# A twelve-layer token mixer in one launch: wide VectorE steps in the rwkv layers, key norms and key factors on ScalarE, and the closed block of the selective layer left out

## The chip, the cores and the metric

One core of a Trainium2 chip. The metric is the device time in microseconds of one execution of the whole program, median over the runs.

## The reference, cut to what matters

The input is 256 tokens of 1024 channels. Twelve sublayers follow one another, each adding its result to `x`: rwkv, ffn, stick-breaking attention, ffn, selective attention ("dsa"), ffn, rwkv, ffn, and then twice a mixed attention ("multi") and a gated ffn. Every sublayer begins with an RMS norm. All of it is float32.

```python
def rms_norm(x, g):
    y = xf * lax.rsqrt(jnp.mean(xf * xf, axis=-1, keepdims=True) + RMS_EPS)
    return (y * g).astype(x.dtype)

# rwkv, the parts that the change touches
shifted = jnp.pad(h, ((0, 0), (1, 0), (0, 0)))[:, :-1]
xm = h[:, :, None, :] + (shifted - h)[:, :, None, :] * mix        # six mixes
kk = heads(k * k_k)
kk = kk * lax.rsqrt(jnp.maximum(jnp.sum(kk * kk, axis=-1, keepdims=True), 1e-24))
k = k * (1.0 + (a - 1.0) * k_a)

# selective attention, 64 queries at a time
visible = kpos[None, :] < ((qpos // 64 + 1) * 64)[:, None]
score = sum over 8 index heads of wi * relu(qi . ki)              # where visible
top_val, top_idx = lax.top_k(score, 64)
p = softmax(q . k over the chosen keys);  o = p . v
```

The first 128 queries can see only the first 128 keys. So one block of 128 queries by 128 keys of every score matrix of the selective layer is closed.

## The kernel before, in words

Activations lie with channels on the 128 partitions, as eight tiles of 256 tokens. A "unit" is one weight block of 128x1024 that SyncE loads into a ring of four (`ring_a`). ScalarE writes its rounded high half (`hi`, L2026) and VectorE the remainder (`lo`, L2135) to `w_split`, and TensorE multiplies the unit in 24 matmuls: high by high, high by low, low by high, for eight tiles of channels (L1931 to L1933, in the rwkv layer's unit 0 L288 to L290, output units of attention L1353 to L1355). Each engine has its program written out in order; semaphores join them. The order by hand decides everything: an instruction waits until all those before it on its engine are through.

**Norm of an rwkv layer.** ScalarE squares the eight tiles of `x` (L2049), TensorE sums all eight with a matrix of ones (L1918), ScalarE takes ln and exp for the inverse root (L2034, L2036), VectorE multiplies `x` by gain and inverse root, tile by tile (L2148). GpSimd subtracts each token from its predecessor (L1142, L1143). VectorE forms the mixes in pairs of tiles (L868), ScalarE the high half of a pair (L639), VectorE the low half (L875). TensorE takes unit 0 pair by pair as they come. The waits for the large constant table stand behind this norm on TensorE, ScalarE and VectorE.

**Key norms.** While units 0 to 7 (the keys) run, ScalarE squares them. TensorE gathers sums by head (L297). ScalarE takes the square root (L657), with a table of its own, then the tanh of the decay ranks (L659), the high halves of mix pairs 2 and 3, and the ranks' high half (L665). VectorE clamps (L912) and inverts (L914); TensorE spreads the result back later. Unit 9 waits for the four pairs of group 3; the small matmuls of the decay (L319 to L321) wait for the ranks.

**Key factors.** After the gates, VectorE forms `1 + (a - 1) * k_a` and multiplies the keys, two instructions per tile of channels (L989, L992), with three unit splits between them.

**The selective layer.** 30 units are projected in "slots", then eight output units follow in slots 30 to 42. In slot n TensorE runs unit n and then what the pairs of heads need by then: norm and rope of queries and keys (L1271, L1273), turning values (L1280), scores (L1296), turning probabilities (L1309), the value product (L1320). In a slot VectorE does, in this order: index rope, normalise the first head of a pair, rope norms, shift and take maxima of a score pair (L1706, L1712), unit splits, normalise the second head (L1718, L1722), the low half of a pair's output (`out_low`, L1729), index sums, the top-eight steps, and last the evacuation of unit n (L1630). Eight steps, each two maxima of eight and two replacements (L1682, L1686), make the 64 chosen keys: one each in slots 9 to 14, with a second one in 10 and 13; the mask follows in slot 14. ScalarE squares a head pair (L1475, L1476) once its unit is evacuated. A later unit shares its PSUM bank with a value product, so it waits for `out_low` of that pair. Scores, probabilities and index scores are 512 columns: two blocks of 128 queries by 256 keys.

## Time and profile before

| | us |
|---|---|
| median of 3 runs | 2387.6 |
| lowest, highest | 2386.41, 2393.24 |
| the profiled execution | 2389.38 |
| its span, first to last instruction | 2387.6 |
| mean granted TensorE clock | 0.98 of full |

The profile is of one execution. PE is TensorE's matmuls, PEld its weight loads, DVE VectorE, ACT ScalarE, POOL GpSimd, SP SyncE. The profile names an instruction by engine and line, then the tile that it writes and those that it reads. In brackets stands how long the engine sat idle before it, and what released it.

### The profile page before, as it was taken

How to read it: one execution, taken by the hardware profiler on the slowest of the kernel's cores; microseconds unless marked ns; L12 is line 12 of the kernel's file. 1: busy time of each engine (PE TensorE's matmuls, PEld its weight loads, DVE VectorE, ACT ScalarE, POOL GpSimd, SP SyncE). 2: the span in 40 equal slices, each digit the busy share in tenths (PEclk: the TensorE clock that was granted, in tenths of full speed). 3: DMA queues.
4: the chain of work that ended last, by engine and by line, in shares of the span. 5: the costliest groups of instructions: out<-in, count | busy, mean ns of one | idle time of the engine just before them, and what ended most of it. 6: DMA issues, size and time to landing. Idle time of an engine off the chain costs nothing.

```text
span 2387.6 us, 55688 instructions
## 1 busy us (share of the span) xinstructions
PE 2251.9 (94%) x23028; PEld 2156.6 (90%) x23028; DVE 1568.9 (66%) x2402; ACT 1207.9 (51%) x2037; POOL 58.1 (2%) x83
## 2 busy tenths in 40 slices
PE   6899899999999989899988998999998999998998
PEld 5799799999999978799978998999897999887998
DVE  6854465566655688565588644655775777775776
ACT  5633454465544546454467334544675444675443
POOL 1000000000000010000010000000000000100000
PEclk8999999999999999999999999999999999998999
DMA  5310265533555433255523102555433554433653
GB/s 198 124 47 4 68 211 172 193 124 124 173 196 171 155 99 106 98 185 189 172 98 124 47 4 98 194 184 177 135 114 107 180 199 150 150 116 101 205 173 118
DMA packets 88437, 327.21 MB, mean 137 GB/s; under 512 B 9809, under 2 KB 9937, under 8 KB 87633
## 3 DMA queue, kind: packets, MB, share of 16 engines
q1 hardware_dynamic: 87984, 322.72, 40.2%
q8 instruction: 128, 2.10, 0.4%
q0 software_dynamic: 288, 2.10, 0.3%
q14 instruction: 37, 0.29, 0.0%
HBM read 323.73 MB, written 1.05 MB: 136 GB/s over the span
## 4 chain that ended last, share of the span: by engine, by line
PE 81%; DVE 10%; ACT 6%; issue 2%; ACTq 0%; DVEq 0%
PE bank L1931 15%; PE bank L1932 15%; PE bank L1933 15%; PE bank L1953 5%; PE bank L1954 5%; PE bank L1955 5%; DVE w_split L2135 2%; ACT w_split L2026 2%; PE bank L446 2%; PE bank L455 2%; PE bank L1353 1%; PE bank L1354 1%; PE bank L1355 1%; PE bank L469 1%; PE bank L1320 1%
## 5 line engine op out<-in xcount | busy, mean ns | idle before, releaser
L1931 PE MATMUL bank<-h_split,w_split 128*128 128x256 f32 x3176 | 912.2, 287 | 20.9 <-DVE h_split L2157 8.0
L1933 PE MATMUL bank<-h_split,w_split 128*128 128x256 f32 x3176 | 898.0, 283 | 0.0
L1932 PE MATMUL bank<-h_split,w_split 128*128 128x256 f32 x3176 | 897.9, 283 | 0.0
L2135 DVE TENSOR_TENSOR w_split<-ring_a,w_split 128x1024 fp32r<-128x1024 f32 x474 | 568.3, 1224 | 191.8 <-ACT w_split L2026 190.7
L1931 PEld LDWEIGHTS bank<-h_split,w_split 128*128 128x128 f32 x3176 | 602.4, 190 | 33.9 <-DVE h_split L2157 11.3
L1932 PEld LDWEIGHTS bank<-h_split,w_split 128*128 128x128 f32 x3176 | 598.3, 188 | 1.3
L1933 PEld LDWEIGHTS bank<-h_split,w_split 128*128 128x128 f32 x3176 | 597.0, 188 | 0.0
L2026 ACT ACTIVATE w_split<-ring_a 128x1024 fp32r<-128x1024 f32 x474 | 483.3, 1049 | 38.1 <-PE bank L1933 33.0
L1953 PE MATMUL bank<-act_split,d_split 128*128 128x256 f32 x1008 | 285.9, 284 | 3.8 <-DVE act_last L2218 2.4
L1954 PE MATMUL bank<-act_split,d_split 128*128 128x256 f32 x1008 | 285.5, 283 | 0.0
L1955 PE MATMUL bank<-act_split,d_split 128*128 128x256 f32 x1008 | 285.3, 283 | 0.0
L2097 ACT ACTIVATE work<-work 128x256 f32<-128x256 f32 x88 | 36.8, 419 | 347.8 <-DVE work L2196 347.8
L1953 PEld LDWEIGHTS bank<-act_split,d_split 128*128 128x128 f32 x1008 | 193.2, 192 | 5.0 <-DVE act_last L2218 2.8
L1955 PEld LDWEIGHTS bank<-act_split,d_split 128*128 128x128 f32 x1008 | 193.3, 192 | 0.0
L1954 PEld LDWEIGHTS bank<-act_split,d_split 128*128 128x128 f32 x1008 | 193.1, 192 | 0.0
L2196 DVE TENSOR_TENSOR work<-bank,work 128x512 f32<-128x512 f32 x132 | 91.0, 689 | 151.5 <-PE bank L1933 150.7
L2193 DVE TENSOR_TENSOR d_split<-ring_d,d_split 128x1024 fp32r<-128x1024 f32 x126 | 153.7, 1220 | 4.9 <-ACT d_split L2094 4.9
L2094 ACT ACTIVATE d_split<-ring_d 128x1024 fp32r<-128x1024 f32 x126 | 131.4, 1043 | 0.0
L2100 ACT ACTIVATE work<-work 128x256 f32<-128x256 f32 x44 | 18.4, 418 | 179.6 <-DVE work L2210 179.6
L1353 PE MATMUL bank<-o_split,w_split 128*128 128x256 f32 x256 | 80.7, 315 | 18.7 <-DVE o_split L1729 18.5
L2214 DVE TENSOR_TENSOR work<-work 128x256 f32<-128x256 f32 x132 | 56.2, 426 | 63.9 <-ACT work L2097 42.6
L2218 DVE TENSOR_TENSOR act_split<-work,act_split 128x256 fp32r<-128x256 f32 x126 | 53.6, 425 | 61.0 <-ACT act_split L2103 61.0
(273 smaller groups left out, 3263.9 us busy)
## 6 DMA issues: line engine op xcount, KB each, us to landing
ring_a<-wa SPq DMA_DIRECT2D x474, 512.0 KB, 3.9
ring_d<-wd SPq DMA_DIRECT2D x132, 512.0 KB, 4.4
tab_sb<-tab SPq DMA_DIRECT2D x1, 2448.0 KB, 13.4
hT<-na POOLq DMA_DIRECT2D x2, 1024.0 KB, 5.3
xT<-x SPq DMA_DIRECT2D x1, 1024.0 KB, 4.9
out<-xT SPq DMA_DIRECT2D x1, 1024.0 KB, 3.9
vec_sb<-vec SPq DMA_DIRECT2D x1, 288.0 KB, 4.9
tab_sb<-tab SPq DMA_DIRECT2D x1, 65.0 KB, 4.7
```

The source lines that it names most:

```text
L1353: mm(o, w[:, 0, ms], x[:, 0, k, :], start=(k == 0 and m % 2 == 0), stop=False, skip_group_check=True)
L1931: mm(dst, w[:, 0, ks], x[:, 0, k, :], start=(k == 0), stop=False)
L1932: mm(dst, w[:, 0, ks], x[:, 1, k, :], start=False, stop=False)
L1933: last = mm(dst, w[:, 1, ks], x[:, 0, k, :], start=False, stop=(k == KT - 1))
L1953: mm(o, w[:, 0, ms], x[:, 0, :], start=(first and m % 2 == 0), stop=False, skip_group_check=True)
L1954: mm(o, w[:, 0, ms], x[:, 1, :], start=False, stop=False, skip_group_check=True)
L1955: return mm(o, w[:, 1, ms], x[:, 0, :], start=False, stop=final, skip_group_check=True)
L2026: A(w_split[:, u % 4, 0, :], ring_a[:, u % 4, :], ACT.Copy).then_inc(s["w_hi"], 1)
L2094: A(d_split[:, q, 0, :], ring_d[:, q, :], ACT.Copy).then_inc(s["dn_hi"], 1)
L2135: v.tensor_tensor(w_split[:, u % 4, 1, :], ring_a[:, u % 4, :], w_split[:, u % 4, 0, :].bitcast(f32), ALU.subtract).then_inc(s["w_lo"], 1)
L2193: v.tensor_tensor(dd[:, 1, :], ring_d[:, q, :], dd[:, 0, :].bitcast(f32), ALU.subtract).then_inc(s["dn_lo"], 1)
L2196: v.tensor_tensor(work[:, 2 * q:2 * q + 2, :], B[4 + q][:, :].rearrange("p (a b) -> p a b", a=2), inv_rms().unsqueeze(1).broadcast_to([P, ...
```

## The change

- In the first layer alone, VectorE adds the eight squares down to two before TensorE's sum, the log and exp table is loaded ahead of the first wait, and the waits for the large table stand where it is first read.
- In both rwkv layers VectorE multiplies `x` by the gain in eight instructions that don't wait for the root. Then it multiplies by the inverse root and subtracts the shifted tokens in wide instructions over half of the channels (1024 columns); GpSimd has no part in these layers.
- The key sums are clamped by VectorE out of PSUM, and ScalarE makes the inverse root by ln and exp. The two mix pairs that stood behind the tanh now stand before it.
- ScalarE makes the key factor (`a * k_a + (1 - k_a)`), VectorE multiplies the keys in two wide instructions.
- The selective layer leaves out the closed block: index scores, scores, probabilities and their turned copies are 384 columns wide. The maximum is taken in two instructions per head. `out_low` moves ahead of the unit splits, the evacuation ahead of the top-eight steps, and these run in slots 9 to 15, two of them in slot 10; the mask is made in slot 15.

The diff, cut to its core (not shown: the same column ranges in the index sums, exp, normalisation and turned copies, and semaphore names):

```diff
@@ -308,6 +308,7 @@
             mixed(1)
             product(B[0][:, 0:S], split_of(8), x_split[1]).then_inc(s["lora1_mm"], 1)
+            pe.wait_ge(s["tab_loaded"], 16)
             for n in range(KT):
                 pe.wait_ge(s["kk_sq"], 8 * r + n + 1)
...
@@ -651,14 +652,14 @@
                 act.wait_ge(s["a_used"], u + n + 1)
                 A(extra[:, n, :], B[4 + n % 4][:, 0:S], ACT.Square, scale=V(f"k_k_{j}", n)).then_inc(s["kk_sq"], 1)
                 evac(n, n, 8 + n)
-            xm_hi(3, 0)
-            xm_hi(3, 1)
-            act.wait_ge(s["kk_sum"], r + 1)
-            A(kk_sums, B[2][:, :], ACT.Sqrt).then_inc(s["kk_std"], 1)
+            for p in range(4):
+                xm_hi(3, p)
+            act.wait_ge(s["kk_std"], r + 1)
+            step.did(A(kk_sums, kk_sums, ACT.Ln))
+            step.settle()
+            A(kk_sums, kk_sums, ACT.Exp, scale=-0.5).then_inc(s["kk_inv"], 1)
             act.wait_ge(s["lora1_mm"], r + 1)
             step.did(A(work[0:64, 4, :], B[0][0:64, 0:S], ACT.Tanh))
-            xm_hi(3, 2)
-            xm_hi(3, 3)
             act.wait_ge(s["a_used"], u + 9)
...
@@ -735,8 +736,18 @@
                 A(gate[:, n, :], B[p][:, 0:S], ACT.Copy).then_inc(s["gate_ready"], 1)
             for n in range(8):
                 gates(n)
+
+            def key_factor(n):
+                A(qkv[:, n, :], qkv[:, n, :], ACT.Identity, bias=small[:, 56 + n:57 + n], scale=V(f"k_a_{j}", n))\
+                    .then_inc(s["kf_ready"], 1)
+            act.wait_ge(s["a_read"], r + 1)
+            act.wait_ge(s["ka_rest"], r + 1)
             split(25)
+            for n in range(4):
+                key_factor(n)
             split(26)
+            for n in range(4, 8):
+                key_factor(n)
             for m in range(1, 8):
                 evac_r(m)
...
@@ -851,7 +862,20 @@
         def rwkv_dve(dve, L, v, step, lo, add_out):
             r, j, u = L["rw"], L["idx"], L["u"]
-            dve.wait_ge(s["h_raw"], 8 * (r + 1))
+
+            def scaled(h):
+
+                step.settle()
+                t = hT[:, 4 * h:4 * h + 4, :]
+                v.tensor_tensor(t, t, inv_rms().unsqueeze(1).broadcast_to([P, 4, S]), ALU.mult)\
+                    .then_inc(s["h_raw"], 1)
+
+            def shifted(h):
+
+                dve.wait_ge(s["h_raw"], 2 * r + h + 1)
+                t, d = hT[:, 4 * h:4 * h + 4, :], sq[:, 4 * h:4 * h + 4, :]
+                v.tensor_tensor(d[:, :, 1:S], t[:, :, 0:S - 1], t[:, :, 1:S], ALU.subtract)
+                v.tensor_scalar(d[:, :, 0:1], t[:, :, 0:1], -1.0, None, ALU.mult).then_inc(s["xx_ready"], 1)
             def low(n):
...
@@ -889,11 +915,21 @@
                                        in1=B[n % 4][:, n // 4 * S:(n // 4 + 1) * S], op0=ALU.mult, op1=ALU.mult)\
                     .then_inc(s["kk_done"], 1)
+            scaled(0)
+            shifted(0)
             mixed(0, 0)
-            for p in range(1, 5):
-                if p < 4:
-                    mixed(0, p)
-                mixed_low(0, p - 1)
+            mixed(0, 1)
+            mixed_low(0, 0)
+            scaled(1)
+            mixed_low(0, 1)
+            shifted(1)
+            mixed(0, 2)
+            mixed(0, 3)
+            mixed_low(0, 2)
+            mixed_low(0, 3)
+            v.tensor_scalar(small[:, 56:64], V(f"k_a_{j}"), -1.0, 1.0, ALU.mult, ALU.add).then_inc(s["ka_rest"], 1)
+            if L["part"] == 0:
+                low(2)
             for n in range(8):
                 mixed(1 + n // 4, n % 4)
...
@@ -902,16 +938,15 @@
             for p in range(1, 5):
                 if p < 4:
                     mixed(3, p)
+                if p == 2:
+                    dve.wait_ge(s["kk_sum"], r + 1)
+                    v.tensor_scalar(kk_sums, B[2][:, :], 1e-24, None, ALU.max).then_inc(s["kk_std"], 1)
                 mixed_low(3, p - 1)
             low(11)
             dve.wait_ge(s["lora1_hi"], r + 1)
             v.tensor_tensor(work_r[:, 4, :], work[:, 4, :], work_r[:, 7, :].bitcast(f32), ALU.subtract)\
                 .then_inc(s["lora1_ready"], 1)
             low(12)
-            dve.wait_ge(s["kk_std"], r + 1)
-            step.did(v.tensor_scalar(kk_sums, kk_sums, 1e-12, None, ALU.max))
-            step.settle()
-            v.reciprocal(kk_sums, kk_sums).then_inc(s["kk_inv"], 1)
             v.memset(dec[:, :, 0:1], 1.0).then_inc(s["dec_edge"], 1)
             for m in range(8):
...
@@ -960,9 +995,13 @@
             else:
                 dve.wait_ge(s["a_used"], u + 18)
             for h in range(2):
-                step.did(v.tensor_tensor(half_rows(oT, h), rows(0, h), rows(24, h), ALU.mult))
+                ins = v.tensor_tensor(half_rows(oT, h), rows(0, h), rows(24, h), ALU.mult)
+                if h == 0:
+                    step.did(ins)
+            ins.then_inc(s["a_read"], 1)
             low(24)
             step.settle()
+            dve.wait_ge(s["a_read"], r + 1)
             if j:
...
@@ -984,17 +1023,10 @@
                 last.then_inc(s["v_final"], 1)
             low(25)
             low(26)
-            for n in range(KT + 1):
-                if n < KT:
-                    step.did(v.tensor_scalar(work[:, n % 4, :], qkv[:, n, :], 1.0, V(f"k_a_{j}", n), ALU.subtract, ALU.mult))
-                if n:
-                    step.settle()
-                    last = v.scalar_tensor_tensor(out=qkv[:, 7 + n, :], in0=work[:, (n - 1) % 4, :], scalar=1.0,
-                                                  in1=qkv[:, 7 + n, :], op0=ALU.add, op1=ALU.mult)
-                    if n < KT:
-                        step.did(last)
-                if n in (3, 6):
-                    low(26 + n // 3)
+            for h in range(2):
+                dve.wait_ge(s["kf_ready"], 8 * r + 4 * h + 4)
+                last = v.tensor_tensor(rows(8, h), rows(8, h), rows(0, h), ALU.mult)
+                low(27 + h)
             last.then_inc(s["k_done"], 1)
             low(29)
...
@@ -1134,14 +1166,6 @@
                                 rw_o_split[:, 0, o, tok(3)].bitcast(f32), ALU.subtract).then_inc(s["o_ready"], 4)
             add_out(L, 30)
-        def rwkv_pool(pool, L, pstep):
-
-            r, g_ = L["rw"], nc.gpsimd
-            for k in range(KT):
-                pool.wait_ge(s["h_raw"], 8 * r + k + 1)
-                g_.tensor_tensor(sq[:, k, 1:S], hT[:, k, 0:S - 1], hT[:, k, 1:S], ALU.subtract)
-                g_.tensor_scalar(sq[:, k, 0:1], hT[:, k, 0:1], -1.0, None, ALU.mult).then_inc(s["xx_ready"], 1)
-
...
@@ -1173,10 +1197,16 @@
             return qkv[:, 16 + t, :]
         hT_flat = hT[:, :, :].rearrange("p a b -> p (a b)")
-        index_scores, top8 = hT_flat[:, 0:512], hT_flat[:, 512:528]
+        def keys_of(kind, qt):
+
+            if kind == "dsa":
+                return slice(0, P) if qt == 0 else slice(P, 3 * P)
+            return slice(qt * S, (qt + 1) * S)
+
+        index_scores, top8 = hT_flat[:, 0:3 * P], hT_flat[:, 512:528]
         def index_relu(i):
-            return hT_flat[:, 1024 + (i % 2) * 512:1536 + (i % 2) * 512]
+            return hT_flat[:, 1024 + (i % 2) * 512:1024 + (i % 2) * 512 + 3 * P]
         halves = planes[:, 4:6, :].rearrange("p a b -> p (a b)")
...
@@ -1293,7 +1323,8 @@
                 for qt in range(NT):
                     for e in range(2):
                         h = slice(HD * e, HD * e + HD)
-                        last = mm(B[e][:, qt * S:(qt + 1) * S], qkv[h, t, qt * P:(qt + 1) * P], qkv[h, 8 + t, :],
+                        keys = slice(0, (qt + 1) * P if kind == "dsa" else S)
+                        last = mm(B[e][:, keys_of(kind, qt)], qkv[h, t, qt * P:(qt + 1) * P], qkv[h, 8 + t, keys],
...
                 p_ = probs(t, e)
+                if kind == "dsa":
+                    for b in range(3):
+                        last = nc.tensor.transpose(B[3][:, b * P:(b + 1) * P], p_[:, b * P:(b + 1) * P], T("ident"))
                 for st in range(NT):
-                    for qt in range(NT):
+                    for qt in range(NT if kind == "multi" else 0):
...
                         h = slice(HD * e, HD * e + HD)
-                        last = mm(pv_bank(L, t)[h, :], v_pair(t)[:, st * P + HD * e:st * P + HD * e + HD],
-                                  turned(e)[:, st * S:(st + 1) * S], start=(st == 0), stop=(st == NT - 1),
+                        a = P if kind == "dsa" and st else 0
+                        last = mm(pv_bank(L, t)[h, a:S], v_pair(t)[:, st * P + HD * e:st * P + HD * e + HD],
+                                  turned(e)[:, st * S:(st + 1) * S - a], start=(st == 0), stop=(st == NT - 1),
                                   skip_group_check=True)
...
@@ -1800,6 +1844,9 @@
                 t = pair_at(L, n, 7 + lag)
                 if t is not None:
                     shifted(t)
+                t = pair_at(L, n, 11 + lag)
+                if t is not None and kind == "dsa":
+                    out_low(t)
                 if kind == "multi" and n in (18, 27):
                     segment(n // 9 - 2)
                 if kind == "multi" and n == 28:
...
@@ -1810,26 +1857,24 @@
                 t = pair_at(L, n, 8 + lag)
                 if t is not None:
                     normed(2 * t + 1)
-                t = pair_at(L, n, 11 + lag)
-                if t is not None and kind == "dsa":
-                    out_low(t)
                 if kind == "multi" and n == 19:
                     segment_low(0)
                 if kind == "dsa":
                     if 5 <= n <= 8:
                         index_add(2 * n - 10)
                         index_add(2 * n - 9)
+                if n < N:
+                    evac(n)
+                if kind == "dsa":
                     if n == 9:
                         dve.wait_ge(s["idx_added"], IDX_HEADS)
-                    if 9 <= n <= 14:
+                    if 9 <= n <= 15:
                         take_eight()
-                    if n in (10, 13):
...
+                    if n == 10:
                         take_eight()
-                    if n == 14:
+                    if n == 15:
                         step.did(v.tensor_scalar(index_scores, index_scores, TAKEN / 2, NEG, ALU.is_gt, ALU.mult))
                         step.settle()
-                if n < N:
...
@@ -1912,7 +1957,11 @@
             def norm(L):
                 m = L["part"]
-                if L["kind"] == "rwkv":
+                if m == 0:
+                    pe.wait_ge(s["first_summed"], 1)
+                    for k in range(2):
+                        last = mm(norm_bank(m)[:, 0:S], T("ones"), sq[:, k, :], start=(k == 0), stop=(k == 1))
...
@@ -2015,6 +2062,7 @@
         def _(act):
             A = nc.scalar.activation
             step = Steps(act, s["act_step"])
+            nc.scalar.preload_act_table_set("natural_log_exp_and_others")
             act.wait_ge(s["const_loaded"], 32)
...
                 if L["kind"] == "rwkv":
+                    if m == 0:
+                        hi(L, 0)
+                        hi(L, 1)
                     root(L)
                 else:
                     if not after_mixer:
@@ -2061,8 +2112,7 @@
                             squares(b)
                     root_table()
                 if m == 0:
-                    for n in range(early(L)):
-                        hi(L, n)
...
@@ -2141,15 +2189,24 @@
             def norm(L):
-                rms_inverse(L)
+                if L["part"] == 0:
+                    for b in range(1, 4):
+                        dve.wait_ge(s["sq_ready"], 2 * b + 2)
+                        if b > 1:
+                            step.settle()
+                        ins = v.tensor_tensor(sq[:, 0:2, :], sq[:, 0:2, :], sq[:, 2 * b:2 * b + 2, :], ALU.add)
+                        if b < 3:
+                            step.did(ins)
+                        else:
+                            ins.then_inc(s["first_summed"], 1)
+                dve.wait_ge(s["x_added"], 8 * (L["part"] + 1))
+                for k in range(KT):
+                    last = v.tensor_scalar(hT[:, k, :], xT[:, k, :], V(gain_of(L), k), None, ALU.mult)
+                step.did(last)
                 if L["part"] == 0:
                     lo(L, 0)
-                for k in range(KT):
-                    v.scalar_tensor_tensor(out=hT[:, k, :], in0=xT[:, k, :], scalar=V(gain_of(L), k), in1=inv_rms(),
-                                           op0=ALU.mult, op1=ALU.mult).then_inc(s["h_raw"], 1)
-                if L["part"] == 0:
-                    for n in range(1, early(L)):
-                        lo(L, n)
+                    lo(L, 1)
+                rms_inverse(L)
```

## Rows read from the trace of the kernel before

**Rows 1.** First section of the page: busy us, share of span, instructions

```profile
PE 2251.9 (94%) x23028; PEld 2156.6 (90%) x23028; DVE 1568.9 (66%) x2402; ACT 1207.9 (51%) x2037; POOL 58.1 (2%) x83
```

**Rows 2.** Stretches: length, then busy us of each engine, clock, DMA

```profile
12.00:30.00 18.00, 4.19 (x16) 3.18 (x14) 13.37 (x20) 5.62 (x8) 10.64 (x16) 0.63 0.51 192
...
800.00:1016.00 216.00, 187.58 (x1402) 168.87 (x1401) 158.29 (x319) 116.10 (x242) 18.32 (x21) 0.98 0.31 104
```

**Rows 3.** Timeline of TensorE, 0 to 36: start, length, instruction, idle before

```profile
8.43 6.12 PE L1918 MATMUL bank<-sq,tab_sb 128*128 128x256 f32 x16 [8.43 <-ACT sq L2049]
28.16 0.55 PE L288 MATMUL bank<-h_split,w_split 128*128 128x256 f32 x1 [13.60 <-DVE h_split L875]
...
34.06 0.28 PE L1931 MATMUL bank<-h_split,w_split 128*128 128x256 f32 x1
```

**Rows 4.** Timeline of ScalarE, first layer's norm

```profile
7.87 2.56 ACT L2049 ACTIVATE sq<-xT 128x256 f32<-128x256 f32 x8
14.59 0.47 ACT L2034 ACTIVATE work<-bank,tab_sb 128x256 f32<-128x256 f32 x1 [4.17 <-PE bank L1918]
```

**Rows 5.** Timeline of VectorE, mixes beside GpSimd and without it

```profile
24.62 2.37 DVE L868 SCALAR_TENSOR_TENSOR work<-sq,vec_sb,hT 128x256 f32<-128x256 f32 x4
...
34.08 0.69 DVE L875 TENSOR_TENSOR x_split<-work,x_split 128x512 fp32r<-128x512 f32 x1
34.68 0.88 DVE L868 SCALAR_TENSOR_TENSOR work<-sq,vec_sb,hT 128x256 f32<-128x256 f32 x2
```

**Rows 6.** Groups by shape: count, then busy us, mean ns, idle

```profile
L963 DVE TENSOR_TENSOR oT<-qkv 128x1024 f32<-128x1024 f32 x4 | 4.7, 1219 | 0.0
```

**Rows 7.** Timelines of ScalarE, VectorE, TensorE, 57 to 67

```profile
57.36 1.28 ACT L657 ACT_TABLE_LOAD   x1
58.66 0.60 ACT L657 ACTIVATE work<-bank 128x512 f32<-128x512 f32 x1
...
62.42 0.42 ACT L665 ACTIVATE work_r<-work 128x256 fp32r<-128x256 f32 x1
...
66.89 3.35 DVE L914 RECIPROCAL work<-work 128x512 f32<-128x512 f32 x1
...
62.84 0.39 PE L1931 MATMUL bank<-h_split,w_split 128*128 128x256 f32 x1 [1.54 <-DVE h_split L875]
```

**Rows 8.** Timelines of VectorE and TensorE, second rwkv layer's norm

```profile
1207.64 4.32 DVE L2148 SCALAR_TENSOR_TENSOR hT<-xT,vec_sb,work 128x256 f32<-128x256 f32 x8 [3.42 <-ACT work L2036]
...
1215.42 0.55 PE L288 MATMUL bank<-h_split,w_split 128*128 128x256 f32 x1 [8.77 <-DVE h_split L875]
...
1221.82 0.28 PE L1931 MATMUL bank<-h_split,w_split 128*128 128x256 f32 x1
```

**Rows 9.** Groups of 800 to 1016, and the top-k slots as one stretch

```profile
L1271 PE MATMUL bank<-dec,tab_sb 128*128 128x256 f32 x32 | 10.6, 412 | 10.7 <-ACT dec L1476 10.7
...
L1682 DVE MAX8 hT<-hT 128x8 f32<-128x256 f32 x16 | 6.0, 415 | 0.1
...
858.00:893.00 35.00, 24.26 (x179) 22.32 (x179) 28.44 (x76) 13.39 (x26) 6.42 (x4) 1.00 0.28 91
```

**Rows 10.** The steady slots: group, timelines of VectorE and ScalarE, one stretch

```profile
L1931 PE MATMUL bank<-h_split,w_split 128*128 128x256 f32 x273 | 81.8, 300 | 7.6 <-issue 4.7 <-DVE h_split L2157 2.9
...
914.01 0.41 DVE L1729 TENSOR_TENSOR o_split<-bank,o_split 128x256 fp32r<-128x256 f32 x1
...
910.36 0.36 ACT L1510 ACTIVATE o_split<-bank 128x256 fp32r<-128x256 f32 x1
...
914.52:930.19 15.67, 14.11 (x106) 12.38 (x107) 11.68 (x24) 9.73 (x24) 1.28 (x2) 1.00 0.31 100
```

**Rows 11.** Groups of 800 to 1016: shifted scores and their matmuls

```profile
L1706 DVE SCALAR_TENSOR_TENSOR planes<-bank,hT 128x512 f32<-128x512 f32 x16 | 10.3, 685 | 13.0 <-PE bank L1296 13.0
...
L1296 PE MATMUL bank<-qkv 64*128 64x256 f32 x64 | 9.1, 402 | 0.0
```

**Rows 12.** The same groups: the output projection's matmuls

```profile
L1353 PE MATMUL bank<-o_split,w_split 128*128 128x256 f32 x64 | 20.1, 314 | 5.4 <-DVE o_split L1729 5.4
```

64 lines of the change are left out of this document (34 added, 30 removed).

## The prediction

> **What bounds the kernel now.** I read the page first: TensorE is busy for 94% of the span, VectorE 66%, ScalarE 51%, GpSimd 2% [rows 1]. A change that touches neither the products nor the weights can then only win where TensorE stands idle, where it runs at half clock, and where its own small matmuls are too wide. So I went by stage through busy time and granted clock, then through TensorE's timeline for every row with an idle time in brackets, and for each asked which VectorE or ScalarE instruction released it. Three places stand out. The start: in 12 to 30 us TensorE is busy 4.2 of 18 us at a clock of 0.63 [rows 2], and before unit 0 it idles 13.6 us [rows 3]. The second rwkv layer: 8.8 us idle ahead of unit 0 [rows 8]. The selective layer (800 to 1016): 187.6 of 216 us busy [rows 2], the holes being waits for the squares of the head norm, 10.7 us between 861 and 894 [rows 9], one wait of 1.56 us every 15.7 us, 4.7 in three [rows 10], and waits for the low half of an attention pair, 5.4 us [rows 12]. The profiled execution took 2389.4 us for a span of 2387.6 us; the median of the three runs is 2387.6 us. I sum against 2389.4 and subtract the same difference from the median.
>
> **The change, part by part.**
>
> *Start of the first rwkv layer.* Before: a table load of 1.28 us stands behind the wait for the constants (6.6), eight squares follow from 7.87 and take 2.56 us, TensorE sums them in 16 passes of 6.12 us, the root starts at 14.59 and takes 0.9 us [rows 3, 4]. VectorE then splits unit 0, takes 4.3 us for eight norm products (as in rows 8), two more splits, and the first mixes at 24.62 run beside GpSimd, whose 16 instructions are 10.6 us of work [rows 2, 5]. After: the table load moves ahead of the wait, so the squares run 6.6 to 9.2. VectorE folds the eight squares to two: three adds of 512 columns, the last 0.7 us after the last square, about 10.1. TensorE has two matmuls, 4 passes of the 16, 6.12/4 = 1.5 and latency: 11.9. Root: 12.9. Beside this VectorE does the eight gain multiplies (under 0.3 each, hidden) and splits of units 0 and 1 (1.2 each, to 14.1; ScalarE has converted both by 11.3). Then one wide product of 1024 columns 1.22 [rows 6], one wide shift 1.2 plus a column of 0.1, two mix pairs 0.8 each, the first low half 0.7 [rows 5]: 14.1+1.2+1.3+1.6+0.7 = 18.9 to 19.1, against 28.16. The other half: product 1.2, low 0.7, shift 1.3, two mixes 1.6, two lows 1.3, so the last low half ends near 25.2. Unit 0 then needs six more matmuls at 0.12 to 0.21: 26.1 to 26.5, against 34.0 [rows 3], 7.5 us. The clock takes some back: before, it rose 5.7 us after TensorE had begun at 28.16. If it rises as long after 24.4, where unit 0 resumes after a 2 us hole, unit 1 runs at 1.2 GHz and costs up to 2.2 us more. I take -7.3, bounds -9 and -5. The weights can't hold it back by much: the four first units are issued before the large table, and ScalarE took the first three without a pause.
>
> *Second rwkv layer.* Sum and root are as before (end 1207.6). Removed: 4.3 us of norm products [rows 8] and GpSimd's chain. Added after the root: 1.2+1.3+1.6+0.7 = 4.9, so unit 0 starts at 1212.6 rather than 1215.42; the last low half ends at 1218.3 and unit 0 at 1219.0 (clock up) to 1220.4 (clock down), against 1221.8. I take -1.8, bounds -3.0 and -0.3.
> The row of the mixes beside GpSimd (24.62, 2.37 us for four) stands against two pairs at 0.88 each without it (34.68) [rows 5]: GpSimd's reads slow VectorE. The Trainium skill, "SBUF — State Buffer", section "SBUF: two separate sides", says the two take turns on an exclusive lock when VectorE has two SBUF inputs; the trace agrees, and by that rule too the move ends the slowing.
>
> *Key norms.* Removed: square-root table load 1.28, Sqrt 0.6, clamp, reciprocal 3.35 [rows 7]. Added: a clamp from PSUM on VectorE among the mixes of group 3, 0.65 (between 0.4 and 0.75, the 512-column rows), and Ln and Exp of 0.6 each on ScalarE, in the table that is loaded. The 3.35 us go from VectorE, but VectorE then waits for ScalarE's sigmoids anyway, so they are worth nothing to the end. What counts: ScalarE converts all four mix pairs first, so the 1.54 us wait at 62.84 [rows 7] shrinks to 0.4. But Ln, Exp, the Tanh table and Tanh now stand behind the fourth pair: 61.0+1.2+1.3+0.4+copy 0.4+copy 0.4 = 64.7 for the high half of the decay ranks, against 62.84 [rows 7]. The unit 11 split, the low half and the sigmoids behind it come 1 to 1.8 us later; TensorE stops after unit 9 and the 1.1 us gained is returned and more; later waits of 0.5 and 1.1 us absorb part. I take +0.6 per layer, bounds -0.7 and +1.7: +1.2 for two.
> The Trainium skill, "ScalarE: Activation LUTs", section "What ACT_TABLE_LOAD costs", puts a switch at 1283 ns plus a drain of about 1380 ns. Here Sqrt starts 0.02 us after its load's 1.28 us ends [rows 7]; the measurement decides, 1.28 per load. By the page the two removed loads would give another 1.4 us each.
>
> *Key factors.* 16 small VectorE instructions per layer become 2 wide ones and 8 ScalarE ones between the splits of units 25 and 27. TensorE has no idle row in this stretch; units are split 3 us or more ahead. 0, bounds -0.5 and +1 (unit 25 or 27 late).
>
> *Selective layer, order.* A unit's evacuation now precedes the top-eight step. That step is 1.7 us (two maxima of 0.415, a little overlapped, and two replacements as long, with their loads) and there are eight, 16 maxima, in slots 9 to 15 [rows 9]. ScalarE's square waits for the evacuation, and TensorE's norm for the square: these are 2.15, 3.06, 2.15, 3.07 and 0.24, five of them, 10.7 in all [rows 9]. They can't all go, since VectorE becomes the bound: seven slots hold seven splits and evacuations (10.8), five rope norms (6.9), eight top-eights (11.4 when a quarter narrower) and the mask, 29.5 us and some waits for ScalarE, against about 25.5 of TensorE. Walking through the slots in order I find unit 18 starting at 892.6 instead of 898.7: -6.1, bounds -2 and -9.
> The low half of an attention pair now goes before the splits and the second normalisation. TensorE's wait of 1.56 ahead of 914.52 is one of three that the profile puts down to nothing ("issue", 4.7), but the low half runs 914.01 to 914.42, and its high half was ready from 910.72 [rows 10]. VectorE has a free place at 911.2. With the wait ahead of the first output unit, 1.61 us, that makes 6.3: -6.3, bounds 0 and -6.3. The other 3.8 of the 5.4 us in front of output units [rows 12] are 1.72, 1.01 and 1.03; the first two are of the same sort, the last has nothing in front of the low half: -2.5. The layer's mean clock is 0.98 [rows 2]: two stretches of 3.4 us behind such waits run at half clock, about 15 matmuls each at 0.21 instead of 0.12. -1.5 if one of them goes, bounds 0 and -2.7.
>
> *Selective layer, width.* 128 of 512 columns go. On VectorE 685 ns for 512 and 1219 for 1024 make 0.13 us for 128 [rows 6, 11], but 16 reductions become 32, so the reductions save next to nothing. On TensorE eight score passes with 0.4 us each overlap to 1.1 us [rows 11]; a quarter of the columns is 0.25, the same for the value product and 0.2 for eight transposes that become six: 0.7 per pair, 8 pairs, and 0.25 for each of four index pairs. 6.6 in all; the first pairs hide behind VectorE, the last are a chain of latency. -5, bounds -2 and -7.
>
> Layer total -6.1-6.3-2.5-1.5-5 = -21.4; because these all assume that nothing else is next in line, I take -20, bounds -10 and -27.
>
> **Sum.** -7.3-1.8+1.2+0-20 = -27.9. 2389.4 - 27.9 = 2361.5 profiled; the median goes from 2387.6 to about 2360.
>
> **Rivals.** (a) *VectorE stays the bound of the selective layer.* The order alone moves waits about, and only the narrower work counts. For it: 28.4 us of VectorE in the 35 us of the top-k slots leave little [rows 9]. Against: the steady slots have 4.0 us of slack in 15.7 [rows 10]. Then the layer gives -9 and the sum is -17: 2371.
> (b) *All of it comes,* half-clock stretches included, and both starts at their best: -27-9-3+1 = -38: 2350.
> (c) *The start is not VectorE's chain but the clock:* short bursts of unit 0 between the wide steps keep TensorE at 1.2 GHz through several units. A unit of 24 matmuls then takes 5.1 us instead of 2.9, 2.2 more. Four units late: 2369.
> (d) *Slower than before,* the same mechanism in the selective layer: pauses return in every slot of a narrower TensorE and the granted clock falls there. 30 units at 2.2 us are +66 and the sum +38 (2426); it decides from 13 units on. For it: pauses of 1.0 and 2.9 us stand beside half-clock stretches. Against: 858 to 893 holds four pauses of 2.2 to 3.1 us at a clock of 1.00 [rows 9]. The Trainium skill, "TensorE: Matmul & The Clock Gate", section "HAM oscillation — how this bites in real kernels", tells of exactly such re-throttling between short bursts; the trace doesn't bear it out for pauses this far apart.
> (e) *The key norms cost more:* Ln and Exp bring two table loads of their own in each layer, 2.6 us each: 2365.
>
> **How the numbers follow.** Forecast 0.62, (a) 0.17, (b) 0.11, (c) 0.05, (e) 0.03, (d) 0.02. The range takes in (b) nearly and (a): 2349 to 2374. A difference under 0.3% (7 us) can't be told from none: faster, below 2380.4: 0.94; same: 0.04, out of (a) and (c), if the selective layer gives nothing and the start half; slower: 0.02, which is (d).
>
> **What would show it.** Right: unit 0 of the first layer starts near 19 and ends near 26.5; in the second it starts 5 us after the root; no idle row of 1.5 us per three units in the selective layer, and its length down from 197 (813 to 1010) to about 177; TensorE waits about 2 us for the decay ranks after unit 9. Wrong: unit 0 ends after 30, waits of 2 to 3 us remain in all top-k slots, or granted clock under 0.97 in the selective layer.

## The result, and the profile after

The changed kernel takes 2365.07 us (median of 4 runs, 2361.32 to 2365.70) against 2390.42 us for the kernel before (4 runs, 2386.41 to 2394.53). The ratio is 0.9894, 95% interval 0.9872 to 0.9916: faster by 1.1%, where 2360 had been forecast (2349 to 2374). The profiled execution took 2364.49 us for a span of 2362.4, 25.2 us shorter than the span before; its mean granted clock is 0.984 against 0.980.

The first section of the page, against [rows 1]: TensorE loses 8.6 us of work, the rest of the 25 us were pauses. GpSimd keeps only its part in the attention layers.

```profile
PE 2243.3 (95%) x23000; PEld 2152.0 (91%) x23000; DVE 1553.5 (66%) x2405; ACT 1210.1 (51%) x2053; POOL 34.1 (1%) x51
```

**Start of the first rwkv layer.** TensorE's timeline of the changed kernel, then ScalarE's and VectorE's, against [rows 3 to 5]:

```profile
10.73 2.04 PE L1963 MATMUL bank<-sq,tab_sb 128*128 128x256 f32 x4 [10.73 <-DVE sq L2197]
19.88 0.55 PE L288 MATMUL bank<-h_split,w_split 128*128 128x256 f32 x1 [7.11 <-DVE h_split L899]
...
25.12 0.58 PE L288 MATMUL bank<-h_split,w_split 128*128 128x256 f32 x1 [1.94 <-DVE h_split L899]
...
27.84 0.41 PE L1980 MATMUL bank<-h_split,w_split 128*128 128x256 f32 x1
...
29.26 0.28 PE L1981 MATMUL bank<-h_split,w_split 128*128 128x256 f32 x1
```

```profile
6.93 2.56 ACT L2097 ACTIVATE sq<-xT 128x256 f32<-128x256 f32 x8 [4.90 <-DVE small L2176]
...
13.32 0.42 ACT L2084 ACTIVATE work<-work 128x256 f32<-128x256 f32 x1
```

```profile
8.30 2.28 DVE L2197 TENSOR_TENSOR sq<-sq 128x512 f32<-128x512 f32 x3 [1.43 <-ACT sq L2097]
10.50 2.19 DVE L2204 TENSOR_SCALAR hT<-xT,vec_sb 128x256 f32<-128x256 f32 x8
12.60 2.35 DVE L2183 TENSOR_TENSOR w_split<-ring_a,w_split 128x1024 fp32r<-128x1024 f32 x2
14.87 1.22 DVE L870 TENSOR_TENSOR hT<-hT,work 128x1024 f32<-128x1024 f32 x1
16.12 1.22 DVE L877 TENSOR_TENSOR sq<-hT 128x1020 f32<-128x1020 f32 x1
...
24.38 1.47 DVE L899 TENSOR_TENSOR h_split<-work,h_split 128x512 fp32r<-128x512 f32 x2
```

Unit 0 starts 8.3 us earlier and stops once for 1.94 us. The root is ready at 13.74 (13.32 + 0.42), but from 10.5 us on VectorE has no idle row: the gain multiplies (2.19 us) and two splits come first, so the wide product starts at 14.87. The matmuls tell the clock: they follow at 0.21 us apiece (0.41 long) until 29.1, at 0.12 after it. TensorE was at 1.2 GHz through all of unit 0 and into unit 1. By the end of the keys 5.6 us of the 8.3 are left: unit 9's wait begins at 55.67 (56.33 - 0.66) against 61.30 (62.84 - 1.54, [rows 7]).

**Key norms.** TensorE, ScalarE and VectorE of the changed kernel behind the keys, against [rows 7]:

```profile
61.96 0.40 PE L320 MATMUL bank<-work_r,w_split 64*128 64x256 f32 x2 [2.49 <-DVE work_r L947]
```

```profile
55.45 0.61 ACT L658 ACTIVATE work<-work 128x512 f32<-128x512 f32 x1
56.10 0.63 ACT L660 ACTIVATE work<-work 128x512 f32<-128x512 f32 x1
56.75 1.28 ACT L662 ACT_TABLE_LOAD   x1
58.04 0.38 ACT L662 ACTIVATE work<-bank 64x256 f32<-64x256 f32 x1
58.44 0.38 ACT L664 ACTIVATE work<-bank 64x256 f32<-64x256 f32 x1
58.85 0.42 ACT L666 ACTIVATE work_r<-work 128x256 fp32r<-128x256 f32 x1
59.18 1.99 ACT L2074 ACTIVATE w_split<-ring_a 128x1024 fp32r<-128x1024 f32 x2
```

```profile
52.67 0.69 DVE L943 TENSOR_SCALAR work<-bank 128x512 f32<-128x512 f32 x1
...
60.25 1.22 DVE L2183 TENSOR_TENSOR w_split<-ring_a,w_split 128x1024 fp32r<-128x1024 f32 x1 [3.97 <-ACT w_split L2074]
61.39 0.42 DVE L947 TENSOR_TENSOR work_r<-work,work_r 128x256 fp32r<-128x256 f32 x1
```

Read the last fence with the one above it. The ranks' high half is ready at 59.27. VectorE is idle, but next in its program stands the split of unit 11, which waits for ScalarE until 60.25; only then come the ranks. TensorE, through with unit 9 at 59.5, stands still for 2.49 us, and from 63.3 to 66.7 us it runs at half clock. The second layer has the same wait (2.49 at 1226.02). The kernel before has the same order on VectorE, and there it costs nothing: the low half, which ends at 65.38, is there before TensorE is through with unit 9 near 66.

```profile
64.96 0.42 DVE L908 TENSOR_TENSOR work_r<-work,work_r 128x256 fp32r<-128x256 f32 x1
```

The stretch from the end of unit 8 to the start of unit 15, in which the two kernels do the same products (units 9 and 11 to 14 and the small ones between them; columns as in [rows 2]), first before, then after. The expectations below call its end "unit 13"; counted in the order of TensorE's program it is unit 15.

```profile
61.30:83.28 21.98, 19.83 (x185) 18.40 (x185) 19.68 (x28) 17.10 (x33) 0.00 (x0) 1.00 0.29 96
```

```profile
55.67:80.37 24.70, 21.07 (x185) 19.73 (x185) 15.31 (x25) 19.10 (x35) 0.00 (x0) 0.93 0.27 86
```

VectorE has 4.4 us less to do and TensorE comes out 2.7 us later.

**Selective layer.** Stretches between the same waits in both kernels: whole layer, and from the first output unit to its end; before, then after.

```profile
815.89:1009.07 193.18, 165.82 (x1226) 147.73 (x1227) 141.46 (x292) 102.43 (x219) 18.32 (x21) 0.98 0.32 106
...
961.59:1009.07 47.48, 38.30 (x278) 33.27 (x279) 24.74 (x49) 19.50 (x46) 0.00 (x0) 0.93 0.29 98
```

```profile
809.99:980.39 170.40, 157.22 (x1210) 142.72 (x1211) 135.08 (x308) 97.93 (x219) 14.36 (x21) 0.99 0.36 120
...
894.00:941.00 47.00, 47.00 (x371) 43.07 (x368) 40.25 (x90) 33.81 (x88) 5.10 (x8) 1.00 0.35 116
942.04:980.39 38.35, 32.17 (x253) 28.34 (x254) 21.99 (x51) 17.32 (x45) 0.00 (x0) 0.96 0.32 111
```

22.8 us less: 8.6 of TensorE's busy time (one half-clock stretch of 3.4 us fewer is in it) and 14.2 of its pauses. From 894 to 941 TensorE is busy without a gap (47.00 of 47.00), where before a wait of 1.56 us stood every 15.7 us [rows 10]. The groups of 794 to 985 show what is left, against [rows 9, 11, 12]: 3.5 us of waits for the head norm's squares (10.7 before) and 2.1 in front of output units (5.4). The 3.7 us in front of the turning of probabilities, for VectorE's normalisation, are not less than before (3.3).

```profile
L1388 PE MATMUL bank<-o_split,w_split 128*128 128x256 f32 x64 | 19.6, 306 | 2.1 <-DVE o_split L1773 1.4 <-DVE qkv L1696 0.6
...
L1301 PE MATMUL bank<-dec,tab_sb 128*128 128x256 f32 x32 | 10.6, 412 | 3.5 <-ACT dec L1511 3.5
...
L1743 DVE SCALAR_TENSOR_TENSOR planes<-bank,hT 128x384 f32<-128x384 f32 x16 | 8.1, 550 | 5.7 <-PE bank L1327 5.7
```

### The profile page after: what moved, and what is told of

It reads as the page before. It is cut to its first block, busy times and chain, and to the rows that moved or that the text cites. A ratio compares the mean times of both kernels' runs of the same rounds, so it can differ in the third digit from the quotient of the medians.

```text
span 2362.4 us, 55626 instructions
## 1 busy us (share of the span) xinstructions
PE 2243.3 (95%) x23000; PEld 2152.0 (91%) x23000; DVE 1553.5 (66%) x2405; ACT 1210.1 (51%) x2053; POOL 34.1 (1%) x51
## 4 chain that ended last, share of the span: by engine, by line
PE 82%; DVE 10%; ACT 6%; issue 2%; DMA 0%; SPq 0%; ACTq 0%; DVEq 0%
PE bank L1980 16%; PE bank L1981 15%; PE bank L1982 15%; PE bank L2002 5%; PE bank L2003 5%; PE bank L2004 5%; DVE w_split L2183 2%; ACT w_split L2074 2%; PE bank L447 2%; PE bank L456 2%; PE bank L1388 1%; PE bank L1389 1%; PE bank L470 1%; PE bank L1390 1%; PE bank L398 1%
## 5 line engine op out<-in xcount | busy, mean ns | idle before, releaser
L1980 PEld LDWEIGHTS bank<-h_split,w_split 128*128 128x128 f32 x3176 | 604.2, 190 | 26.5 <-DVE h_split L2214 11.3
```

The lines of the kernel that those rows point to most:

```text
L1980: mm(dst, w[:, 0, ks], x[:, 0, k, :], start=(k == 0), stop=False)
```

## The experiments

All were timed beside the kernel before on the same chip. That kernel's own runs spread over 10 us and more (2384.7 to 2397.2 in the first set), and its median differs from set to set (2389.06, 2394.33 and 2392.08 us), so the parts are judged by their stretches in the profile first and by the times second. "Stretch" is always the one from the end of unit 8 to the start of unit 15: 21.98 before, 24.70 changed.

**The ranks' low half first** (`e1_ranks_first`, on the changed kernel)

```diff
-            low(11)
             dve.wait_ge(s["lora1_hi"], r + 1)
             v.tensor_tensor(work_r[:, 4, :], work[:, 4, :], work_r[:, 7, :].bitcast(f32), ALU.subtract)\
                 .then_inc(s["lora1_ready"], 1)
+            low(11)
```

> The changed kernel with one move on VectorE in both rwkv layers: the low half of the decay ranks is formed ahead of the split of unit 11 instead of behind it. In the trace of the changed kernel the ranks' high half is ready at 59.27 us, but VectorE first waits 3.97 us for ScalarE's half of unit 11 and splits it (60.25 to 61.47), so TensorE waits 2.49 us at 61.96; 1226.02 is the same, and each wait is followed by 3.4 us at half clock. Theory K (the key norms cost more than forecast because the ranks' low half is queued behind a split that itself waits): the low half ends near 59.7, the wait shrinks to under 0.5 us in each layer, -2.0 each, and -1.0 more each if the half-clock stretch goes: 4 to 6 us under the changed kernel's 2365, a ratio to before of about 0.987. Rival L (the wait only moves one unit on, to unit 11, whose split now ends later): under 1 us, 2364 to 2366, with a new wait of about 2 us in front of unit 11. Rival C (the loss in this stretch is the clock's and comes back in another place): the wait goes, but half-clock stretches of the same total length stand elsewhere, and 2363 to 2366.

2359.89 us (2357.95 to 2365.81), ratio 0.9879 (0.9858 to 0.9900). TensorE and VectorE of this kernel:

```profile
60.20 0.39 PE L320 MATMUL bank<-work_r,w_split 64*128 64x256 f32 x2 [0.41 <-DVE work_r L946]
```

```profile
59.62 0.43 DVE L946 TENSOR_TENSOR work_r<-work,work_r 128x256 fp32r<-128x256 f32 x1 [3.03 <-ACT work_r L666]
60.57 2.36 DVE L2183 TENSOR_TENSOR w_split<-ring_a,w_split 128x1024 fp32r<-128x1024 f32 x2 [0.52 <-ACT w_split L2074]
```

```profile
55.99:78.80 22.81, 19.99 (x185) 18.41 (x185) 15.39 (x25) 19.12 (x35) 0.00 (x0) 1.00 0.27 93
```

The wait falls from 2.49 to 0.41 us and the half-clock stretch behind it is gone (clock 1.00, was 0.93). The stretch is 1.9 us shorter here and in the second layer (22.78); of the 1.9, 1.1 is TensorE's busy time (21.07 against 19.99), which is the half clock, and 0.8 is pauses. Theory K holds; rival L does not, no new wait stands ahead of unit 11. Rival C the times can't exclude: two of the five runs are as long as the changed kernel's, and half clock falls differently in every execution. Waits of 0.74 and 0.48 us appear for ScalarE's sigmoids instead, so not all of the 2.7 comes back.

**The old key norms** (`e2_old_keynorm`, on the changed kernel: the hunks at -651 and -902 of the diff reversed)

> The changed kernel with the key norms of before: square root on ScalarE with its table load, two mix pairs behind the tanh, clamp and reciprocal of 3.35 us on VectorE. Read from the two traces, the stretch from the end of the keys to unit 13 lasts 21.98 us before (61.30 to 83.28) and 24.70 after (55.67 to 80.37); in the second layer it is the same. Theory K (the new key norms cost 2.7 us a layer, where +0.6 was forecast): both stretches go back to 22.0, 5.4 us in all, 2359 to 2361, ratio about 0.987; a wait of 1.54 us ahead of unit 9 is back, none at the ranks. Rival (the wait at the ranks comes from the earlier start of the layer, not from the new key norms): it stays, and the time is 2364 to 2368, the reciprocal costing on top.

2361.89 us (2357.10 to 2365.23), ratio 0.9875 (0.9855 to 0.9895), between what theory K and the rival had said; the times don't decide, the stretch does.

```profile
55.20:77.19 21.99, 19.83 (x184) 18.40 (x185) 19.67 (x28) 17.10 (x33) 0.00 (x0) 1.00 0.30 96
```

21.99, and 22.00 in the second layer: to 0.02 us what the kernel before had, with the layer starting 8.3 us earlier. The wait at the ranks is gone. It belongs to the new key norms, not to the earlier start.

**The new key norms alone** (`e3_keynorm_only`, the same two hunks put on the kernel before)

> The kernel before with the new key norms alone. Theory K: +2.7 us a layer, about 2395 against 2390, ratio 1.001 to 1.003; TensorE's wait ahead of unit 9 falls from 1.54 to about 0.7 us and a wait of about 2.5 us stands at the decay ranks. My forecast on record would be +0.6 a layer, ratio 1.0005. Rival (the reciprocal's 3.35 us on VectorE were on the path): faster by 2 us or more, ratio under 0.999.

2396.72 us (12 runs, 2394.26 to 2403.59), ratio 1.0030 (1.0017 to 1.0043): this part by itself makes the kernel slower, by 4 to 10 us in time and by 2 x 2.7 in the profile:

```profile
61.29:86.00 24.71, 21.08 (x184) 19.75 (x185) 15.29 (x25) 19.11 (x35) 0.00 (x0) 0.93 0.27 86
```

**The start alone** (`e4_start_only`: on the kernel before, `scaled`, `shifted` and the new order of mixes, the folded squares, the table load ahead of the first wait, the gain ahead of the root and the moved waits)

> The kernel before with the start of the rwkv layers alone: gain ahead of the root, wide products and shifts on VectorE, squares folded first, waits for the large table moved; old key norms, key factors and selective layer. The two traces put the gain by the end of the keys at 5.6 us in the first layer and 0.6 us in the second. Theory S (that is all): -6.2 us, ratio 0.9974. Theory P (the first layer's later half-clock stretches, 102 to 109 and 115 to 123 us in the trace before and only 3.4 us after, fall away with the shift): about -10 us, ratio 0.996. Rival (the clock gives it all back, since unit 0 is torn apart): under 2 us, ratio 0.999 to 1.000.

2387.04 us (13 runs, 2377.70 to 2391.70), ratio 0.9985 (0.9973 to 0.9996). Theory S, 0.9974, lies at one edge of the interval, theory P, 0.996, outside; the rival's 0.999 lies inside, so the times don't tell S from it. The profile does: the wait of unit 9 begins at 53.96, 7.3 us earlier than before, and in the second layer the gain is 0.7 us, as in the changed kernel. But the profiled execution is the fastest of the 13 by 6.9 us, and its matmuls are at 0.12 us apiece from 25.1 on, 4 us earlier than in the changed kernel, so the 7.3 are more than is usual.

**Order and width of the selective layer apart** (`e5_order_only`: the hunks at -1800 and -1810 on the kernel before; `e6_width_only`: all other hunks of that layer and the mask table on it)

> The kernel before with only the new order on VectorE in the selective layer (low half of a pair ahead of the splits, evacuation ahead of the top-eight steps, these in slots 9 to 15), all of it still 512 columns wide. From one anchor in both traces to the other (815.89 to 1009.07 before, 809.99 to 980.39 after) the layer takes 193.2 us before and 170.4 after. Theory O (the order carries most of it): the four waits of 2.15 to 3.07 us for the head norm's squares shrink to two of 1 to 2 us (-6), the four of 1.6 us in front of units go (-6.3), one of the waits in front of output units goes (-1.7): -14, the layer near 179, ratio 0.994. Rival a (VectorE is the bound there, so the order only moves waits and the narrower work counts): -6 or less, the layer at 187 or more. Rival (order and width need each other: with top-eights of 1.7 us instead of 1.36 the evacuations come late again): the waits of 1.6 go and those for the squares stay, -7 to -9.

> The kernel before with only the closed block of the selective layer left out (384 columns instead of 512 in index scores, scores, probabilities and their turned copies), the order as before. Theory O: the narrower matmuls and transposes give 0.7 us a pair where TensorE has no wait of its own, and shorter VectorE steps shorten the waits a little: -5 to -7 us, ratio 0.9975. Rival a: the layer is bound by VectorE, whose waits shrink with every narrower step: -10 us or more, ratio under 0.996. Rival (what is taken from TensorE's columns comes back as longer waits, since the low half and the squares come no earlier): under 2 us, ratio over 0.999.

2373.12 us (2371.84 to 2374.30), ratio 0.9917 (0.9904 to 0.9930), and 2378.77 us (2376.84 to 2379.25), 0.9937 (0.9925 to 0.9949). The layer in the order kernel, then in the width kernel, there with the steady slots (914.52 to 961.59 before, 47.07) and the output units:

```profile
813.86:993.18 179.32, 163.60 (x1226) 146.77 (x1227) 143.09 (x292) 102.22 (x219) 14.43 (x21) 0.99 0.34 114
```

```profile
815.94:998.44 182.50, 161.11 (x1210) 145.29 (x1211) 134.04 (x308) 98.14 (x219) 18.26 (x21) 0.97 0.34 112
...
910.22:955.14 44.92, 40.38 (x313) 35.95 (x313) 33.39 (x76) 27.98 (x70) 3.82 (x6) 1.00 0.32 105
955.14:998.44 43.30, 34.59 (x271) 30.55 (x272) 23.18 (x55) 18.07 (x46) 0.00 (x0) 0.96 0.31 109
```

The order gives 13.9 us, as theory O said; the width gives 10.7, nearly twice what theory O said. The sum, 24.6, is what both give together (168.4 to 170.4 in eight profiles, 22.8 to 24.8 less): neither needs the other.

The order's 13.9 are not all where theory O had them. In the top-k slots 11.0 us of waits became 7.7, not 5: those for the squares fell to 4.3, but one for an evacuation grew from 0.32 to 1.47 and one of 1.90 for the second normalisation is new. In the output units 2.7 us of waits went instead of 1.7, and one half-clock stretch went.

Of the width's 10.7, 2.2 are in the steady slots (0.7 a pair, the forecast's figure), 4.2 in the output units (one half-clock stretch fewer is in them), and 4.3 in the slots before 910, though two half-clock stretches of 3.4 us stand there that the kernel before doesn't have. There VectorE is busy for 77.5 us instead of 81.6, and the four waits for the squares are 5.6 us together instead of 10.4. That is the mechanism of rival a, beside the order and not in its place.

The times say more than the profiles: the two ratios together would make 35 us, where the whole change gives 25. In this set nine of the ten runs of the kernel before took 2392.7 to 2395.1 us at a mean clock of 0.975 or 0.976, while 12 of the 23 in the first set took under 2389.1. So 0.9917 and 0.9937 are taken as signs only, and the stretches as the measure.

**Sigmoids ahead of the split of unit 13** (`e7_ranks_rates`, on `e1_ranks_first`, ScalarE)

```diff
             evac(9, 8, 16)
-            split(13)
             for n in range(4):
                 rates(n)
+            split(13)
```

> The changed kernel with the ranks' low half ahead of the split of unit 11 on VectorE, as in the last run of that, and the split of unit 13 on ScalarE moved behind the first four pairs of sigmoids of the decay. With the first move alone the stretch from the end of the keys to unit 13 went from 24.70 to 22.81 us, and TensorE then waited 0.74 and 0.48 us for these sigmoids (65.79, 67.25), in front of which ScalarE splits unit 13. Theory K: both waits go, the stretch is 21.8 us or less in both layers (22.0 before), so -5.8 us to the changed kernel, 2358 to 2360 where the clock is the same. Rival: unit 13 is then split too late and TensorE waits about 1 us in front of it, 22.6 to 23; 2360 to 2362.

2360.49 us (2358.36 to 2363.07), ratio 0.9863 (0.9847 to 0.9879). The stretch is 22.32 and 22.31 us: half a microsecond gained, not one. One wait for the sigmoids goes, the other shrinks to 0.33, and VectorE's split of unit 15 comes later, a wait of 0.95 instead of 0.47. The rival had the place two units too early and the price too high.

**Unit 0 held until all four mix pairs are there** (`e8_unit0_held`, on the changed kernel)

```diff
+                    pe.wait_ge(s["xm_ready"], 24 * r + 4)
                     for p in range(4):
-                        pe.wait_ge(s["xm_ready"], 24 * r + p + 1)
```

> The changed kernel, but TensorE begins unit 0 of both rwkv layers only when all four mix pairs are ready (the order of VectorE and ScalarE is untouched). In the changed kernel it starts at 19.88 us, stops for 1.94 us at 25.12 and ends near 26.6. Theory S (what the early start gives is the work done before the last half, a unit of 24 matmuls at 1.2 GHz taking 5.1 us, and the clock rises about as early): unit 0 ends near 30.3, +3 to +4 us in each layer, 2370 to 2373 against 2365, ratio 0.992. Rival c (the torn start keeps the clock down, and one piece without a hole gets it up sooner): no loss, 2363 to 2367, ratio 0.989 or better, with the clock up less than 5 us after unit 0 begins.

2365.43 us (2363.27 to 2372.71), ratio 0.9893 (0.9877 to 0.9909): in time not to be told from the changed kernel. In the profile unit 0 starts at 25.99 and the matmuls are fast from 30.4, 4.4 us later (9.2 in the changed kernel). So the clock did what rival c said (up less than 5 us after unit 0 begins), but the start is not free: unit 8 ends at 58.12 instead of 55.67, and in the second layer 2.1 us later from its sum. In these profiles each early start is worth 2.1 to 2.5 us, less than theory S said. The intervals of the two ratios are wide enough for 4.6 us in all, so the times don't contradict this.

**The changed kernel again, and a version without the clamp** (`e9_changed_again`; `e10_ln_from_psum`, both moves above and the clamp gone, which changes that part of the computation; `e11_ln_scan`, in addition four scans behind the split of unit 15)

```diff
-            act.wait_ge(s["kk_std"], r + 1)
-            step.did(A(kk_sums, kk_sums, ACT.Ln))
+            act.wait_ge(s["kk_sum"], r + 1)
+            step.did(A(kk_sums, B[2][:, :], ACT.Ln, bias=T("kk_eps")[:, 0:1]))
...
-                if p == 2:
-                    dve.wait_ge(s["kk_sum"], r + 1)
-                    v.tensor_scalar(kk_sums, B[2][:, :], 1e-24, None, ALU.max).then_inc(s["kk_std"], 1)
```

> The changed kernel once more, untouched, as the measure for the two runs beside it. If its 4 runs so far (2361.3 to 2365.7) are typical, 2361 to 2368 and the same waits at the same places, while the half-clock stretches behind them differ in number and length; the selective layer, 170.4 us from anchor to anchor in its first profile, is 168.4 where none of it falls in the output units.

> The changed kernel with both moves of the last run of that kind (ranks' low half first, split of unit 13 behind four pairs of sigmoids), and in addition ScalarE takes ln out of PSUM with 1e-24 as its bias, so that VectorE's clamp among the mixes of group 3 is gone (the sum plus 1e-24 in place of the larger of the two: that part of the computation is changed). In the changed kernel VectorE's 0.69 us clamp stands between two mix pairs and the last low half ends at 56.27, so TensorE waits 0.66 us ahead of unit 9, and Ln starts 0.65 us later. Theory K (this chain, clamp and ranks, is what the key norms cost): the wait ahead of unit 9 goes and so does the 0.42 at the ranks, the stretch from the end of the keys to unit 13 is 21.3 us or less against 24.70 changed, 22.31 with both moves and 22.0 before; 2356 to 2359. Rival (VectorE's split of unit 15, 0.95 us of wait, catches TensorE a little later and gives half of it back): 21.8, 2358 to 2360.

> As the run before it, and VectorE's second group of four scans of the decay moved behind the split of unit 15 and the low half of a mix pair. With both moves TensorE waited 0.95 us at 78.00 for that split, which VectorE made at 76.66 to 77.85 behind 2.43 us of scans though ScalarE's half was there at 76.28. Theory: this wait falls to 0.5 us or none and the stretch is another 0.4 us shorter in both layers, 2355 to 2358. Rival (the scans are then the last thing that the decays and the removal keys wait for, and a wait of 0.5 to 2 us appears at the spread norms or the value ranks, about 88 us): no gain, 2357 to 2360.

In its second profile the changed kernel has the same waits (0.67 at 56.06, 2.50 at 61.69) and a selective layer of 168.93 us. Side by side on one chip, four runs each: 2365.82 us (2362.80 to 2367.36), 2360.04 (2356.41 to 2362.61) and 2360.40 (2359.61 to 2362.15); ratios 0.9892 (0.9871 to 0.9914), 0.9873 (0.9850 to 0.9896) and 0.9876 (0.9855 to 0.9896). None of the second's four runs is as long as the shortest of the changed kernel, though the intervals of the ratios overlap. By time it can't be told from `e1_ranks_first` and `e7_ranks_rates`; its stretch is the shortest of them:

```profile
55.24:76.97 21.73, 19.92 (x187) 18.41 (x185) 14.68 (x24) 18.45 (x34) 0.00 (x0) 1.00 0.30 97
```

The wait ahead of unit 9 is gone, but 0.47 at the ranks and 0.95 at unit 15 stay, so 21.73, the rival's figure, still 0.25 under the kernel before. In the last kernel the wait at unit 15 is gone, but one of 0.59 stands ahead of unit 16 and the one at the value ranks grows from 1.06 to 1.42: what is gained is given back to 0.01 us. Its rival was right.

## Why the prediction came out right, term by term

| | forecast | measured in the profile |
|---|---|---|
| first layer's start | -7.3 | -5.6 (-5.3 to -7.3 in eight profiles) |
| second layer's start | -1.8 | -0.65 |
| key norms, both layers | +1.2 | +5.4 |
| key factors | 0 | 0.0 |
| selective layer | -20 | -22.8 (to -24.8) |
| half-clock stretches elsewhere | none | -1.5 |
| sum | -27.9 | -25.2 |

In the last row but one stand the two stretches between the parts whose length changed: from unit 15 of the first layer to the selective layer 3.0 us less, with 10.2 us less of half clock, and from unit 15 of the second to the end 1.4 us more, with 3.4 more. The stretch from the selective layer to the second rwkv layer's norm, 193.86 us, is equal in both kernels. That the clock is all of it is not shown.

**The start** was forecast by the right chain. The steps behind the wide product's start took what was said; what failed is "the eight gain multiplies (under 0.3 each, hidden)". They are hidden from TensorE but not from VectorE: 2.19 us at 10.50, with two splits behind them, so the wide product starts at 14.87 instead of 14.1, and unit 0 at 19.88 instead of 19.0. (The root too was later than the 12.9 of the forecast, 13.74, but VectorE was later still.) "Unit 0 then needs six more matmuls" failed as well: the last two low halves come one right behind the other, so all 12 matmuls of the last two pairs stand behind 25.12, at 0.21 us, and unit 0 ends at 28.0, not at 26.1 to 26.5. The rest is the clock. The term is within its bounds. In the second layer the gains are hidden and unit 0 does start 5.1 us after the root (1178.94 to 1184.05), but the last two low halves end 11.1 us after it instead of 10.7, and all of unit 0 runs at half clock (0.41 us a matmul), the dear end of the forecast. Rival c named this mechanism, with more units late than there were.

**The key norms** are the term that failed, outside its bounds of -0.7 to +1.7 a layer. The chain Ln, Exp, table, tanh, two copies was walked correctly, and its end forecast 64.7 us on the clock of the kernel before, 2 us later than there; so was the wait ("TensorE waits about 2 us for the decay ranks", 2.49). Two things weren't priced. "The unit 11 split, the low half and the sigmoids behind it come 1 to 1.8 us later" took the split's place ahead of the ranks' low half as given and did not ask whether VectorE stands idle there; `e1_ranks_first` shows that this order alone costs 1.9 us a layer. And the wait of 2.5 us brought half clock with it, 1.2 us more of TensorE's busy time for the same 185 matmuls; 1.1 of these 1.2 are in the 1.9. The other 0.8 us of the 2.7 stays in `e1_ranks_first`, with waits for the sigmoids. How much of it is owed to Ln and Exp standing ahead of the tanh, which no run moved, is open. Rival e is refuted: Ln and Exp stand at 55.45 and 56.10 without a table load. The Trainium skill, "ScalarE: Activation LUTs", section "What ACT_TABLE_LOAD costs", has a switch followed by a drain of about 1380 ns; here the tanh follows its load after 0.01 us (56.75 + 1.28, then 58.04), so the measurement stands, 1.28 us for a load.

**The key factors** cost nothing: from unit 20, behind a wait of 4.6 us, to the first state step `e8_unit0_held`, with the new factors, takes 46.57 us (103.39 to 149.96), and `e4_start_only`, with the old ones, 46.58 (96.48 to 143.06), both with 5.5 us of it at half clock.

**The selective layer** came out 3 to 5 us better, from two errors of opposite sign. Order: 6.1 + 6.3 + 2.5 + 1.5 = 16.4 forecast, 13.9 measured. The three waits of 1.56 us in the steady slots went entirely, as said; of the fourth, ahead of the first output unit, 0.7 us stays. The top-k slots gave 3.3 us and not 6.1: the walk through them had already used the narrower top-eight, which the order alone doesn't have. Width: 5 forecast, 10.7 measured, for "the first pairs hide behind VectorE" forgot that VectorE's own steps get shorter there. Rival a is refuted as the whole story: the order alone took 13.9 us, where its condition allowed 6 at most. Rival d is refuted: the layer's clock is 0.99.

**What made the total right** is in part luck: the key norms' +4.2 and the starts' +2.9 stand against -2.8 in the selective layer and -1.5 elsewhere. The ways in which the time goes were right, several sizes were not, and they happened to cancel.

## What to carry to other kernels

Less work on an engine with slack does not make its results come earlier; look at what stands next in its program. Here VectorE's work in the stretch fell by 4.4 us and TensorE waited 2.5 us more at one place, because a short step that TensorE needed, and whose input now came 2 us later from ScalarE, was queued behind a long one that itself waited for ScalarE. Before pricing a later signal, check for an idle row of the engine in between, and swap. Price a step that moves from behind a wait to before it as free only if the engine has nothing else to do before the wait ends.

## What the runs showed of the hardware

The same matmuls take 45.6 to 49.8 us between the same two waits, by how long the granted clock is at 1.2 GHz behind a wait of 4.6 us. Changed kernel, first profile; its second profile; the order kernel; the kernel before. Of their times 3.3, 13.3, 5.5 and 11.9 us are at 1.2 GHz:

```profile
100.90:146.53 45.63, 44.93 (x625) 42.45 (x625) 27.53 (x31) 26.39 (x50) 0.00 (x0) 0.96 0.29 94
```

```profile
100.65:150.49 49.84, 49.14 (x624) 46.15 (x625) 27.62 (x31) 26.49 (x50) 0.00 (x0) 0.87 0.26 86
```

```profile
104.85:151.39 46.54, 45.84 (x624) 43.36 (x624) 30.59 (x45) 22.68 (x42) 0.00 (x0) 0.94 0.28 92
```

```profile
103.83:153.13 49.30, 48.60 (x625) 45.76 (x625) 30.59 (x45) 22.68 (x42) 0.00 (x0) 0.88 0.26 87
```

Two profiles of one kernel differ by 4.2 us here, more than the 2.7 us that the key norms cost in a layer. So two profiles are best compared by stretches at a clock of 1.00, and kernels 5 us apart need many runs.

The length of a wait alone does not tell what the clock does behind it. The wait of 2.49 us at the ranks stands in four profiles (the changed kernel twice, `e3_keynorm_only`, `e8_unit0_held`), in both layers, and 3.4 us at 1.2 GHz follow each of these eight times; in the other nine profiles, where it is 0.48 us or less or absent, none follow. But the four waits of 2.15 to 3.07 us in the top-k slots of the kernel before left the clock at 1.00 [rows 9], and in `e6_width_only` waits of 1.76 and 1.88 us at the same places each had 3.4 us at 1.2 GHz behind them.
